# Attention: VectorE subtracts the low parts of transposed tiles from PSUM, GpSimd those of five slabs of weights

## What is computed

```python
def diff_attention(h, cos, sin, w_qkv, w_o, q_gain, k_gain, ..., sub_gain, lambda_init):
    qkv = h @ w_qkv
    ...
    q = partial_rope(rmsnorm(q, q_gain), cos, sin)
    k = partial_rope(rmsnorm(k, k_gain), cos, sin)
    ...
    def attend_block(q_blk):                     # 128 queries of a head, two maps
        s = jnp.einsum('mbhqd,mbhkd->mbhqk', q_blk, k).astype(jnp.float32) * scale
        p = jax.nn.softmax(s, axis=-1)
        a = p[0] - lam * p[1]
        return jnp.einsum('bhqk,bhkv->bhqv', a.astype(v.dtype), v)
    ...
    o = rmsnorm(o, sub_gain) * (1.0 - lambda_init)
    return o @ w_o
```

## Time and profile before

| | |
|---|---|
| median of 3 runs | 1030.07 us |
| the profiled execution | 1029.67 us, of which the span is 1027.9 us |
| TensorE (PE) busy | 984.7 us, 96% |
| VectorE (DVE) busy | 861.0 us, 84% |
| ScalarE (ACT) busy | 485.0 us, 47% |
| GpSimd (POOL) busy | 427.7 us, 42% |
| attention | about 86 to 311 us of the span |

### The profile page before, as it was taken

One profiled execution on the slowest core, in us unless ns is written; L12 is line 12 of the kernel. 1 busy time (PEld: TensorE's weight loads), 2 busy tenths in 40 slices (PEclk: granted clock), 3 DMA queues, 4 the chain that ended last, 5 costly groups with the idle time before them and its releaser, 6 DMA issues.

```text
span 1027.9 us, 12963 instructions
## 1 busy us (share of the span) xinstructions
PE 984.7 (96%) x4724; PEld 807.5 (79%) x4724; DVE 861.0 (84%) x1123; ACT 485.0 (47%) x743; POOL 427.7 (42%) x371
## 2 busy tenths in 40 slices
PE   5999998889899899999999999999999999999998
PEld 4877776666678688888888888898888888888887
DVE  5567889877955999999999987777998999899883
ACT  4525655577745524434345353355443443443520
POOL 5852687565556273664860400252404304124000
PEclk9999999999999999999999999989999999999999
DMA  6423211220123233323332333301333333332202
GB/s 245 143 49 103 62 42 41 65 100 1 49 73 126 82 103 112 111 86 116 90 120 86 102 104 122 119 5 62 103 102 103 103 102 107 102 112 90 70 14 82
DMA packets 52047, 92.76 MB, mean 90 GB/s; under 512 B 8848, under 2 KB 9872, under 8 KB 51984
## 3 DMA queue, kind: packets, MB, share of 16 engines
q1 hardware_dynamic: 45888, 91.24, 27.9%
q10 hardware_dynamic: 6096, 0.69, 0.5%
HBM read 89.82 MB, written 2.10 MB: 89 GB/s over the span
## 4 chain that ended last, share of the span: by engine, by line
PE 76%; DVE 13%; POOL 4%; issue 3%; ACT 2%; DMA 1%; ACTq 1%; SPq 0%; DVEq 0%; POOLq 0%
PE bank L1602 73%; DVE s_nmax L1263 2%; PE bank L1660 2%; DVE s_w_lo L1153 1%; POOL s_o_r L703 1%; DVE s_p L1285 1%; POOL s_oc L706 1%; DVE s_mixc L1283 1%; DVE s_qkn L1215 1%; DVE s_hT_lo L1336 1%; DMA s_raw<-in_attn_w_qkv 1%; DVE s_rt L1219 1%; DVE s_o_ss L1312 1%; DVE s_qk_ss L1202 1%; DVE s_oc L1273 1%
## 5 line engine op out<-in xcount | busy, mean ns | idle before, releaser
L1602 PE MATMUL bank<-s_hT_hi,s_w_hi 128*128 128x512 f32 x512 | 200.8, 392 | 0.0
L1602 PE MATMUL bank<-s_hT_hi,s_w_lo 128*128 128x512 f32 x512 | 199.3, 389 | 0.0
L1602 PE MATMUL bank<-s_hT_lo,s_w_hi 128*128 128x512 f32 x512 | 199.3, 389 | 0.0
L1153 DVE TENSOR_TENSOR s_w_lo<-s_raw,s_w_hi 128x1024 fp32r<-128x1024 f32 x96 | 155.9, 1642 | 13.9 <-ACT s_w_hi L819 7.7
L754 POOL TENSOR_TENSOR s_lt<-s_lbB,s_lbB 128x1024 f32<-128x1024 f32 x14 | 34.1, 2439 | 268.7 <-PE bank L1602 268.2
L1173 DVE TENSOR_TENSOR s_lbB_lo<-s_lbB,s_b_hi 128x1024 fp32r<-128x1024 f32 x64 | 122.6, 1940 | 0.0
L1390 DVE TENSOR_TENSOR s_acc<-s_acc,bank 128x512 f32<-128x512 f32 x168 | 109.3, 681 | 11.0 <-PE bank L1602 10.8
L1602 PE MATMUL bank<-s_b_hi,s_u_hi 128*128 128x512 f32 x288 | 113.2, 393 | 1.9 <-DVE s_a_lo L1378 1.9
L1602 PEld LDWEIGHTS bank<-s_hT_hi,s_w_hi 128*128 128x128 f32 x512 | 96.2, 188 | 20.1 <-issue 0.5
L1602 PEld LDWEIGHTS bank<-s_hT_lo,s_w_hi 128*128 128x128 f32 x512 | 96.2, 188 | 20.0 <-issue 0.5
L1602 PEld LDWEIGHTS bank<-s_hT_hi,s_w_lo 128*128 128x128 f32 x512 | 96.1, 188 | 20.0
(11 more groups left out here) (197 smaller groups left out, 2189.8 us busy)
## 6 DMA issues: line engine op xcount, KB each, us to landing
s_raw<-in_mlp_w SPq DMA_DIRECT2D x64, 512.0 KB, 3.7
s_lbB<-in_mlp_w SPq DMA_DIRECT2D x64, 512.0 KB, 3.3
s_raw<-in_attn_w_qkv SPq DMA_DIRECT2D x24, 512.0 KB, 4.2
s_raw<-in_attn_w_o SPq DMA_DIRECT2D x8, 512.0 KB, 3.2
s_x_nat<-in_x SPq DMA_DIRECT2D x4, 512.0 KB, 8.5
s_x_again<-in_x SPq DMA_DIRECT2D x4, 512.0 KB, 5.0
out<-s_acc SPq DMA_DIRECT2D x8, 256.0 KB, 2.0
s_raw<-in_pool_w SPq DMA_DIRECT2D x4, 256.0 KB, 2.7
```

The source lines that it names most:

```text
L1153: v.tensor_tensor(w_lo[slot][:, cols], raw[k][:], f32(w_hi[slot][:, cols]), ALU.subtract)\
L1602: return nc.tensor.matmul(o, lhsT, rhs, start=start, stop=stop, **kw)
```

## The change

It has three parts. VectorE takes over all 56 low parts of turned tiles and subtracts straight from bank 4, so that ScalarE's second copy and `turn_raw` fall away; a turn of q, k or o has its scale applied in the same instruction. The next turn into bank 4 now waits for `turn_lo_done`, VectorE's subtraction, in place of `turn_kept`. In exchange GpSimd takes the low parts of the 20 pieces of slabs 4 to 8 (`weight_lo`), at the end of the same steps. Third, in a step without filler TensorE does `values` ahead of the extra turn.

```diff
--- before.py
+++ after.py
@@ -101,6 +101,7 @@
 
 SPLIT = {4: (0, 1, 2, 3), 5: (6, 7, 8, 9), 6: (11, 12, 13, 14), 7: (27, 28, 29, 30), 8: (34, 34, 35, 35)}
 LAST = STEPS + 6
+POOL_SPLITS = (4, 5, 6, 7, 8)
 
 
 def turns():
@@ -284,9 +285,9 @@
         u_part_lo = {A11: a11_lo[:], A12: u_lo[:, 2:4, early], A22: u_lo[:, 2:4, later]}
         u_part_lo |= {n: s_lo[:, k, :, :] for k, n in enumerate(S_ORDER)}
 
-        aT_hi, aT_lo, p0, p1, turn_raw, oc, osq, qkT1_hi, qkT1_lo = inside(
+        aT_hi, aT_lo, p0, p1, oc, osq, qkT1_hi, qkT1_lo = inside(
...
@@ -462,6 +463,14 @@
                 return oT[n][:, 0, :], oT[n][:, 1, :]
             return qkT_hi[n % 2][:, "qk".index(what), :], qkT_lo[n % 2][:, "qk".index(what), :]
 
+        def turn_scale(what):
+
+            if what == "map":
+                return 1.0
+            if what == "o":
+                return sub_col[:, 0:1]
+            return qk_col[:, 0:1] if what == "q" else qk_col[:, 1:2]
+
         def piece(slab, k):
 
             if slab < WO0:
@@ -673,22 +682,20 @@
                 g.tensor_tensor(qk_r[:, n % 2, :], qk_v[:, n % 2, :], minus_half[:], ALU.pow)\
                     .then_inc(qk_r_done, 1)
 
-            def turn_lo(what, n):
-                k = TURN_NO[what, n]
-                hi, lo = turn_dst(what, n)
-                pool.wait_ge(turn_kept, k + 1)
-                g.tensor_tensor(lo, turn_raw[:, k % 2, :], f32(hi), ALU.subtract).then_inc(turn_lo_done, 1)
+            def weight_lo(s, k):
+
+                pool.wait_ge(w_hi_done, s * 4 + k + 1)
+                pool.wait_ge(w_lo_done, s * 4 + k)
+                cols = slice(k * PIECE, (k + 1) * PIECE)
+                g.tensor_tensor(w_lo[s % 2][:, cols], raw[k][:], f32(w_hi[s % 2][:, cols]), ALU.subtract)\
+                    .then_inc(w_lo_done, 1)
 
...
-            turn_lo("q", 0)
-            turn_lo("k", 0)
             for i in range(LAST + 1):
-                if i - 1 in EXTRA:
-                    turn_lo(*EXTRA[i - 1])
                 if i >= 7 and (i - 7) % NT == 0:
 
                     h = (i - 7) // NT
@@ -705,14 +712,16 @@
                     o_tile = oc[:, h % 2, :].rearrange("p (t d) -> p t d", t=NT)
                     g.tensor_tensor(o_tile, o_tile, o_rl[:].unsqueeze(2).to_broadcast([P, NT, VD]), ALU.mult)\
                         .then_inc(o_normed, 1)
-                if 2 <= i < STEPS + 2:
-                    turn_lo("map", i - 2)
                 for f in range(F_V):
                     if TAKE[f] + 1 == i:
                         qk_root(2 * NT + f)
                 for f in range(F_V):
                     if TAKE[f] == i:
                         qk_square(2 * NT + f)
+                for s, steps in SPLIT.items():
+                    for k in range(4):
+                        if steps[k] + 1 == i and s in POOL_SPLITS:
+                            weight_lo(s, k)
 
             def norm_sums(m):
 
@@ -893,20 +902,12 @@
                 k = TURN_NO[what, n]
                 hi, _ = turn_dst(what, n)
                 act.wait_ge(turned, k + 1)
-                scale = 1.0
                 if what == "map":
                     if n >= 2:
                         act.wait_ge(pv_done, n - 1)
-                elif what == "o":
-                    scale = sub_col[:, 0:1]
-                else:
-                    if n >= 2:
-                        act.wait_ge(scored, NT * (n - 1))
-                    scale = qk_col[:, 0:1] if what == "q" else qk_col[:, 1:2]
-                a.activation(hi, bank[4][:], ACT.Copy, scale=scale)
-                if k >= 2:
-                    act.wait_ge(turn_lo_done, k - 1)
-                a.activation(turn_raw[:, k % 2, :], bank[4][:], ACT.Copy, scale=scale).then_inc(turn_kept, 1)
+                elif what in "qk" and n >= 2:
+                    act.wait_ge(scored, NT * (n - 1))
+                a.activation(hi, bank[4][:], ACT.Copy, scale=turn_scale(what)).then_inc(turn_kept, 1)
 
             act.wait_ge(rope_reduced, 1)
             a.activation(ropet[:, 2:4, :], ropet[:, 0:2, :], ACT.Sin).then_inc(rope_act, 1)
@@ -1149,6 +1150,8 @@
             def split_lo(s, k, slot):
 
                 dve.wait_ge(w_hi_done, s * 4 + (k + 1))
+                if s == w1_slab(1):
+                    dve.wait_ge(w_lo_done, s * 4 + k)
                 cols = slice(k * PIECE, (k + 1) * PIECE)
                 v.tensor_tensor(w_lo[slot][:, cols], raw[k][:], f32(w_hi[slot][:, cols]), ALU.subtract)\
                     .then_inc(w_lo_done, 1)
@@ -1228,6 +1231,17 @@
                                        ALU.mult, ALU.subtract)\
                     .then_inc(v_lo_done, 1)
 
+            def turn_lo(what, n):
+
+                k = TURN_NO[what, n]
+                hi, lo = turn_dst(what, n)
+                dve.wait_ge(turn_kept, k + 1)
+                if what == "map":
+                    last = v.tensor_tensor(lo, bank[4][:], f32(hi), ALU.subtract)
+                else:
+                    last = v.scalar_tensor_tensor(lo, bank[4][:], turn_scale(what), f32(hi), ALU.mult, ALU.subtract)
+                last.then_inc(turn_lo_done, 1)
+
             for t in range(NT):
                 split_lo(1, t, 1)
             for s in range(AHEAD):
@@ -1243,6 +1257,10 @@
                         split_lo(2, t, 0)
                     if n >= 2 * NT:
                         v_lo_part(0, t, bank[n % 4])
+                    if n == 2 * NT + 1:
+                        turn_lo("q", 0)
+                    if n == 2 * NT + 2:
+                        turn_lo("k", 0)
                 if s == 0:
 
                     dve.wait_ge(lam_loaded, 16 * 4)
@@ -1286,6 +1304,8 @@
                                        ALU.mult, ALU.add).then_inc(a_done, 1)
 
             for i in range(LAST + 1):
+                if i - 1 in EXTRA:
+                    turn_lo(*EXTRA[i - 1])
                 for f in range(F_V, F_Y):
                     if TAKE[f] + 1 == i:
                         v_lo_part(1, f - F_V, bank[6 + f % 2])
@@ -1301,6 +1321,8 @@
                     o_keep((i - 5) // 2)
                 if i < STEPS:
                     maxima(i)
+                if 2 <= i < STEPS + 2:
+                    turn_lo("map", i - 2)
                 if 1 <= i <= STEPS:
                     combine(i - 1)
                 if i >= 7 and (i - 7) % NT == 0:
@@ -1322,7 +1344,7 @@
                         qk_norm(2 * NT + f)
                 for s, steps in SPLIT.items():
                     for k in range(4):
-                        if steps[k] + 1 == i:
+                        if steps[k] + 1 == i and s < POOL_SPLITS[0]:
                             split_lo(s, k, s % 2)
 
             def add_wo(c):
@@ -1653,7 +1675,7 @@
                     pe.wait_ge(qk_ready, 2 * NT * (n // (NH // 2)) + NT * which + NT)
                     src = [qkn[:, n, which, t, :] for t in range(NT)]
                 if k:
-                    pe.wait_ge(turn_kept, k)
+                    pe.wait_ge(turn_lo_done, k)
                 else:
                     pe.wait_ge(h_lo_done, 2 * NT)
                 for t in range(NT):
@@ -1775,9 +1797,12 @@
                     turn("map", i - 2)
                 for part in now[:1]:
                     filler(*part)
+                values_first = not now and 3 <= i < STEPS
+                if values_first:
+                    values(i - 3)
                 if i in EXTRA and i < STEPS:
                     turn(*EXTRA[i])
-                if 3 <= i < STEPS + 3:
+                if 3 <= i < STEPS + 3 and not values_first:
                     values(i - 3)
                 for part in now[1:]:
                     filler(*part)
@@ -1880,7 +1905,7 @@
-            pe.wait_ge(turn_kept, len(TURNS))
+            pe.wait_ge(turn_lo_done, len(TURNS))
```

2 lines of the change are left out of this document (1 added, 1 removed).

## The result

The changed kernel takes 1037.8 us (median of 4 runs, 1036.4 to 1038.4) against 1030.0 (4 runs, 1029.3 to 1031.6): ratio 1.0074, 95% interval 1.0058 to 1.0090. It is slower by 7.8 us, where 1026.4 was forecast, and lies outside the range of 1019 to 1034.

What follows compares the result with a forecast made beforehand. TensorE's idle time in attention was taken as what could be won, with VectorE as full in the first half. Terms -2 - 3 + 1.3 = -3.7 took 1029.67 to 1026.0, median 1026.4 us; range 1019 to 1034.

Steps and rivals of the forecast that it cites:

- What bounds the kernel now: Attention, 76 to 311 us: TensorE idle 22.4 us; VectorE as full as TensorE in the first half, 12.1 us free in the second.
- Then VectorE's balance in the first half is +5.6 - 5 = about 0.: Steps 3 to 17: 17.8 us in, 12.2 us out, blocking down from 13.1 to 8 us; VectorE stays as full as before.
- Blocking in `combine`: First half: GpSimd's long subtractions hold VectorE's `combine` for 8 us, between bounds of 0 and 24 us.
- the coupling: First half: the next turn waits for VectorE, which works in order, so its lateness stops TensorE at once; 4 us added.
- the value tile's wait: First half: TensorE's 3.9 us wait for a value's low part falls under 2 us, its slow matmuls go; -4 us.
- Second half: Steps 18 to 33: nearly no blocking, fewer waits for the mixed map, ScalarE's copy and `o_keep`; sum -3 us.
- `o_keep`: Step 19: ScalarE and VectorE reach it earlier without the second copy, shortening the 1.3 us wait and slow matmuls; -1.5 us.
- ScalarE's copy: Step 21: TensorE's 1.3 us wait for the second copy shrinks, as the values stand ahead of the turn; -0.8 us.
- the mixed map: Second half: TensorE's waits for it, 1.7 us, become 0.7 us shorter.
- The end: Steps 34 to 36: the last head's root begins 3.6 us later, root and product run 1.8 us shorter; +1.3 us.
- the third: Rival, 22%: VectorE becomes the bound in steps 5 to 13, held by long subtractions, some 15 us of blocking; about 1034 us.
- mean of the mix above 1.4 us: Sign that the forecast is wrong: VectorE's mix in the first half takes over 1.4 us in the mean.

Runs made afterwards that it cites:

- e1: The changed kernel with VectorE's low part of q0 placed ahead of the first low part of the values; 1034.0 us, ratio 1.0032 to the kernel before.
- e5: The changed kernel with all weights' low parts left on VectorE and q0's low part early; 1022.0 us, ratio 0.9909 to the kernel before.
- e13: e5 plus eight unused 128x1024 subtractions on GpSimd at the places of slabs 5 and 6; 1031.1 us, ratio 1.0011 to the kernel before.
- e14: e5 plus unused 128x16 powers on GpSimd at the eight places of slabs 5 and 6; 1022.1 us, ratio 0.9925 to the kernel before.
- e8: e1 with each of GpSimd's 20 weight subtractions issued as two of 512 columns; 1032.4 us, ratio 1.0011 to the kernel before.
- e4: e1 with the weights of slab 8 given back to VectorE; 1031.1 us, ratio 1.0003 to the kernel before.

## Why the prediction was wrong, step by step

In short: the prediction put the lead-in at nothing, where it cost 5.3 us. It put what a late VectorE costs TensorE at 4 us in the first half, where 10.6 us of waits came, and it booked the exchange of the weights as a small gain, where it cost 8.7 us up to step 17 (e1 against e5).

**What bounds the kernel now** was read right: the time to win lies where TensorE stands idle, and long waits cost slow matmuls besides. The text used that for what would be won, and not enough for what could be lost.

**The step that was missing: the lead-in, +5.3 us.** The sum began at step 3. The diff has two lines in the projection phase that put q0's and k0's low parts behind other work of VectorE, with `turn` now waiting for them, and the prediction named neither. It said what a wait for an in-order VectorE does to a turn and applied it to the steps alone. e1, with one instruction moved, stands 5.0 us ahead of the changed kernel at step 17.

**"Then VectorE's balance in the first half is +5.6 - 5 = about 0."** The terms were right. Blocking in `combine` was put at 8 us; it measured 15 x (949 - 751) + 15 x (587 - 210) ns = 8.6. Blocking elsewhere was put at nothing, and some 6 us fell there: a piece of the rotary in `qk_norm` takes 2.36 us in place of 0.29, `s_o_v` 2.32 in place of 0.17. But it had been left out of the count for the kernel before as well (13.1 us of 21.8), and VectorE was no fuller than foretold. What failed is the conclusion: the sum of busy time was taken for the pace. It set 12.2 us of subtractions given away against 8 us of holds as if a microsecond of each were worth the same. A subtraction of 1.22 us at the end of a step lies where VectorE has room: e5, with all of them, is 12 us faster than e1. A hold of 1.2 to 2.2 us falls inside the chain mix, `qk_norm`, low part, turn, and TensorE pays it at once, and in steps 6 and 11 again in matmuls at 0.63. Priced by e1 against e5 the weights cost 8.7 us up to step 17 and 10.8 to the last turn (0.9 of it the chance of step 21), where the sum had them as a gain.

**"I price it at 4 us" (the coupling).** This term was mis-sized. Waits for low parts in steps 3 to 17 are 10.6 us in the changed kernel and in e1, the slow matmuls behind them not counted, and 6.6 us in e5. Without GpSimd's pieces the half nevertheless gets 5.6 us shorter, as the value tile's wait and its slow matmuls go (foretold at 4) and, beyond the sum, all of the mix's holds.

**Second half, -3 foretold, -0.4 measured** (steps 17 to 31), and as little in e5, so this is not the weights. `o_keep` gave what was said: step 19 takes 3.14 us in place of 4.72. ScalarE's copy did not: its wait of 1.26 us is gone, but steps 21 and 22 take 10.5 us in place of 10.1. Not priced were the new waits for low parts there (0.69, 0.76 and 0.83 us before three turns), and those for the mixed map rose from 1.7 to 2.9 in the change where 0.7 less was foretold; in e5 they are 1.4.

**The end, +1.3 foretold, +0.9 measured.** Its terms, 1.8 less 0.7, add up to 1.1 and not to 1.3, which changes nothing here. The root starts 4.9 us behind `osq` in place of 1.3, 3.6 later as said, and root and product run at 1.01 and 1.04. The turn waits 2.29 us. That the rest is the same was right within 1 us: 721.0 and 720.0.

**The rivals.** The case that came is the third in kind: its mark was waits for low parts of over 8 us, and they are 17.6. It foretold long subtractions that hold `combine` or `qk_norm` so that the next turn waits for a late VectorE, and this is what the traces show. It also wanted some 15 us of blocking, which is near the 14.8 estimated above for all instructions; but it counted from 8 us in `combine`, where 8.6 came, and it wanted VectorE at its limit, where it is at 84%. Its +4 for the first half is near the +3.0 measured by luck, since it kept the value tile's wait, which went; and its own terms, +4, -3 and +1.3, lead to 1032.4 and not to 1034. The lead-in, which it did not have, made the rest. Of the other signs these held: no second copies, instructions that read a bank at 0.68 to 0.75 us, 20 pieces of 2.37 to 2.92 us. ScalarE is 28 us less busy and not 34; that difference was not looked into. The mark "mean of the mix above 1.4 us" was not reached (0.949): the kernel lost time all the same.

## What to carry to other kernels

Moving work to an idle engine is priced by what it does to the busy one's chain while it runs, not by the busy time that it takes off it: here 24.4 us given away relieved VectorE by 3.5 us and cost about 10. When a resource (a bank here) gets a new releaser, list every place where it is released, also ahead of the loop, and look at what stands before the new releaser in its engine's order. And a long wait of TensorE can be paid twice, as a wait and as slow matmuls behind it. In attention, in these traces, no wait of 1.0 to 1.3 us was followed by a lower clock, waits of 1.33 to 1.64 us sometimes were, and those over 1.9 us mostly, but not always. When two traces are compared step by step, such a stretch of about 1 us should not be read as the work of an edit.

## What the runs showed of the hardware

By e13 and e14 the hold is about streaming, not about GpSimd being busy. In e14 a power of 128x16 runs on GpSimd from 159.24 to 162.14 us, and beside it `s_mixc` (0.21), the mix (0.75) and `qk_norm`'s product (0.68) all run at their lengths alone. The Trainium skill (SBUF — State Buffer, Who interferes with whom) has a VectorE instruction with two SBUF inputs contend with a GpSimd instruction that reads SBUF, for the whole instruction. e13 agrees (2.40 us for the mix beside two subtractions); e14 doesn't: the power reads SBUF and holds nobody in its 2.90 us.

Also small one-input instructions are held: in e13 the `tensor_scalar` of 128x4 that makes `s_o_v` takes 1.82 us in place of 0.17 beside a subtraction that began 0.09 us before it; in the changed kernel it takes 2.32. The prediction gave the sentence of the Trainium skill (SBUF — State Buffer, Who interferes with whom) on instructions with at most one SBUF input without its condition, that they run outside the 2-port perf modes; here stands one that is held, and its mode is in no trace. And halving the pieces (e8) did not halve the harm: 20 of 1.36 us take 26.9 us on GpSimd where 10 of 2.39 take 23.9, and the held time (14.4 us by the same estimate, 14.8 in e1) moves from one instruction of VectorE to several.

TensorE's clock behind waits of different lengths: after a wait of 0.94 us the matmuls keep 0.39 us (granted clock 1.00 over 127 to 131 us of e5); after 2.16 us some run at 0.63 (0.65 over 127.9 to 132.7 of e1), after 2.84 us ten in a row do (0.50 over 175.6 to 181.5 of the changed kernel). The length of the wait does not decide it alone. The turn of a head's output at the end of step 20, with the same wait ahead of it, and the first score matmuls 1.5 us behind it, in e1 and then in e4 (what TensorE does in the 8 us ahead of it is the same in both within 0.02 us):

```profile
230.13 0.66 PE L1682 MATMUL bank<-s_ident,s_oc 128*128 128x128 f32 x4 [1.64 <-POOL s_oc L713]
...
231.59 0.75 PE L1624 MATMUL bank<-s_qkT_hi 64*128 64x512 f32 x2
```

```profile
230.12 0.66 PE L1682 MATMUL bank<-s_ident,s_oc 128*128 128x128 f32 x4 [1.63 <-POOL s_oc L713]
...
231.58 0.50 PE L1624 MATMUL bank<-s_qkT_hi 64*128 64x512 f32 x2
```

And in the changed kernel the clock of the 5 us behind a wait of 2.53 us (199.94) is 1.00. What else decides, no run here shows.
